# Turns of the modulation vectors: two of 128 rows, or four of 64 in pairs, each half into its own bank

## The chip, the cores and the metric

The program runs on one core of a Trainium2 chip. The metric is the device time of one execution in microseconds (us). The kernel before took 2588.03 us, the median of three runs (2587.11 to 2589.22).

## What is computed

Two stacks of two transformer layers run one after the other on 512 tokens of width 1024, in float32. The first stack has two kinds of attention and a squared-ReLU MLP in each layer. The second stack's layers are modulated by vectors that depend only on a condition `c`:

```python
def second_block(x, c, ada_w, ada_b, ...):
    cond = jax.nn.silu(c)
    for i in range(DEPTH):                      # DEPTH = 2
        mod = cond @ ada_w[i] + ada_b[i]        # [1024] @ [1024, 6144]
        sh1, sc1, g1, sh2, sc2, g2 = jnp.split(mod, N_MOD, axis=-1)
        h = modulate(rmsnorm(x, norm1_g[i]), sh1, sc1)
        ...
```

The change touches the product `cond @ ada_w[i]` alone. It has 2 x 6144 results, each a sum over 1024 inputs.

## The kernel before

The instruction streams of the five engines are written out by hand, each in a function of its own, with semaphores between them; every engine works through its stream in order.

**Large matmuls.** The weights of all products are cut into units of 1024 rows and 256 columns. SyncE loads a unit, ScalarE rounds it into `whi`, GpSimd computes the rest `wlo` (L1891), and TensorE makes two tiles of 128 outputs by 512 tokens from it. A tile is 24 matmuls with 512 columns: for each of 8 chunks of the inner dimension L528 (high times high), L529 (weights high, input low) and L530 (weights low, input high). A tile goes into one of the banks 0 to 3 and is read out by ScalarE or VectorE while the next ones run. All these matmuls use all 128 rows of the array. L622 to L624 are the same in products that are laid out by token.

**An MLP** has eight stages of eight tiles each (`MLP_ORDER`): up, up, down, up, down, up, down, down. In an up stage ScalarE takes ReLU and square of a tile (L1135, L1139), VectorE squares it again in float32 (L1598) and computes the low part (L1601). In a down stage VectorE adds a tile to the residual (L1395, L1397).

**The modulation vectors** need nothing of the tokens, so the product with `ada_w` is worked off beside the first stack's two MLPs, in 48 blocks of 256 outputs, 24 blocks in each MLP, one block for every two tiles:

- SyncE loads the block's 1024 x 256 weights into `ada[k % 2]` (one DMA).
- VectorE (`ada_block(k)`, L1560 and L1563) multiplies eight chunks of 128 rows by the entries of the condition, which stand one to a partition, and adds them up in `acc[k % 2]` (128 partitions, 256 columns). Every step waits for the one before.
- The sum over the 128 partitions is still to be made. TensorE (`ada_sums(k)`, L800 to L807) turns each 128 columns of `acc` with a transpose against the identity: two turns of 128x128, side by side into one bank, 7 or 6 in alternation. `after` calls it behind every even tile from tile 4 to tile 50, so between the last matmul of one tile and the first of the next. TensorE waits there until VectorE's eight steps are done, and until the bank has been read.
- VectorE (`ada_out(k)`, L1565 to L1570) reduces the turned columns, 128 elements per result, adds the bias and writes two columns of `MOD`.

On VectorE the order is `ada_block(k)`, then `ada_out(k - 1)`, then the two tiles' own work. `dve_until` and `pe_until` wait for a semaphore only if a value that high hasn't been waited for before.

**Other short instructions of TensorE.** The attention turns its probabilities in pairs at L691: rows 0 to 63 into bank 4 and rows 64 to 127 into bank 5, each turn 64 rows by 128 columns against a 64x64 identity, and multiplies them by the values at L708. L663 and L671 are its scores, matmuls of 64 rows, also in pairs; while the queries of the second attention are being computed, its first steps stand between large tiles. L918 is one transpose of 48 rows between large tiles, L830 are four of 16 rows, all on the same rows of the array.

Of the kernel before, what the change touches and what calls it, by code (L numbers as in the profile page):

```python
# [7 lines left out]
ALU = mybir.AluOpType  # L8
# [4 lines left out]
P = 128  # L13
# [4 lines left out]
UC = 256  # L18
# [115 lines left out]
def body(nc, ctx, t, consts, out):  # L134
    def sem(name):
        return ctx.enter_context(nc.semaphore(name))

    def sb(name, shape, dt=F32, stack=ctx):
        return stack.enter_context(nc.sbuf_tensor(name, shape, dt))

    bank = [ctx.enter_context(nc.psum_tensor(f"bank{i}", [P, 512], F32)) for i in range(8)]
# [6 lines left out]
    ident, ones = sb("ident", [P, P]), sb("ones", [P, P])  # L148
    head_mean, V2 = sb("head_mean", [P, P]), sb("V2", [P, 96])
# [14 lines left out]
    cond, ada_col = sb("cond", [P, 3, KC]), sb("ada_col", [P, 2, 2])  # L164
    MOD = [sb(f"MOD{i}", [P, 48]) for i in range(2)]
    GM = sb("GM", [P, 4, KC])
    acc = [sb(f"acc{i}", [P, UC]) for i in range(2)]
# [75 lines left out]
    with ExitStack() as region:  # L243
# [11 lines left out]
    hi_done, lo_done, ada_step, ada_sum, ada_red, mod_set, gain_set = (  # L255
        sem(n) for n in ("hi_done", "lo_done", "ada_step", "ada_sum", "ada_red", "mod_set", "gain_set"))
# [164 lines left out]
    def tensor_program(pe):  # L421
# [11 lines left out]
        def wait_chunk(f, c):  # L433
            wait_part(f, KC + c if f in HALVED else c)
# [364 lines left out]
        def mlp(m):  # L799
            def ada_sums(k):  # L800

                pe_until.wait_ge(ada_step, 8 * (k + 1))
                if k >= 2:
                    pe_until.wait_ge(mod_set, k - 1)
                for j in range(2):
                    mm = pe.transpose(bank[7 - k % 2][:, j * P:(j + 1) * P], acc[k % 2][:, j * P:(j + 1) * P], ident[:])
                mm.then_inc(ada_sum, 1)  # L807

            def after(stage, o):
                tile = 8 * stage + o  # L810
                if m < 2 and tile >= 4 and tile % 2 == 0 and tile // 2 - 2 < 24:
                    ada_sums(24 * m + tile // 2 - 2)
            for stage, (f, g) in enumerate(MLP_ORDER):
                name, done = f"m{m}{f}{g}", lambda o, stage=stage: after(stage, o)
                if f == "u":
                    fm(name, X, lambda c: wait_chunk(f"m{m}", c), done, halved=f"m{m}" if g == 0 else None)
                else:
                    fm(name, (Hhi[g % 2], Hlo[g % 2]), lambda c, g=g: pe_until.wait_ge(h_lo, 32 * m + 8 * g + c + 1), done,
                       last=f"m{m}" if g == 3 and m < 3 else None)
# [534 lines left out]
    def vector_program(dve):  # L1354
        dve_until = Until(dve)
# [196 lines left out]
        def ada_block(k):  # L1552

            src, a, cd = ada[k % 2], acc[k % 2], cond[:, 2, :]
            dve_until.wait_ge(ada_in[k % 2], 16 * (k // 2 + 1))
            if k == 0:
                dve_until.wait_ge(silu_step, 3)
            if k >= 2:
                dve_until.wait_ge(ada_sum, k - 1)
            dve.tensor_scalar(a[:], src[:, 0, :], cd[:, 0:1], None, ALU.mult).then_inc(ada_step, 1)  # L1560
            for c in range(1, KC):
                dve_until.wait_ge(ada_step, 8 * k + c)
                dve.scalar_tensor_tensor(a[:], src[:, c, :], cd[:, c:c + 1], a[:], ALU.mult, ALU.add).then_inc(ada_step, 1)  # L1563

        def ada_out(k):  # L1565
            layer, col = k // 24, 2 * (k % 24)
            dve_until.wait_ge(ada_sum, k + 1)
            dve.tensor_reduce(ada_col[:, k % 2, :], bank[7 - k % 2][:, 0:UC].rearrange("p (j k) -> p j k", j=2), mybir.AxisListType.X, ALU.add).then_inc(ada_red, 1)
            dve_until.wait_ge(ada_red, k + 1)
            dve.tensor_tensor(MOD[layer][:, col:col + 2], ada_col[:, k % 2, :], V2[:, 48 * layer + col:48 * layer + col + 2], ALU.add).then_inc(mod_set, 1)  # L1570

        def mod_gains():
            dve_until.wait_ge(mod_set, 48)
# [7 lines left out]
        def mlp(m, gate=None):  # L1581
            for stage, (f, g) in enumerate(MLP_ORDER):
                gm = GEMM[f"m{m}{f}{g}"]
                if m == 1 and stage == 7:
                    mod_gains()
                for o in range(KC - 2 * (m < 3 and stage == 7)):
                    tile = 8 * stage + o
                    if m < 2 and o % 2 == 0 and 2 <= tile < 50:
                        ada_block(24 * m + tile // 2 - 1)
                    if m < 2 and o % 2 == 0 and 4 <= tile < 52:  # L1590
                        ada_out(24 * m + tile // 2 - 2)
                    if f == "u":
                        v = 32 * m + 8 * g + o
                        r = tmp[2 + v % 2]
                        dve_until.wait_ge(up_q, v + 1)
                        if v >= 2:
                            dve_until.wait_ge(h_lo, v - 1)
                        dve.scalar_tensor_tensor(r[:], tmp[v % 2][:], 1.0, tmp[v % 2][:], ALU.mult, ALU.mult).then_inc(up_r, 1)  # L1598
                        dve_until.wait_ge(h_hi, v + 1)
                        dve_until.wait_ge(up_r, v + 1)  # L1600
                        dve.scalar_tensor_tensor(Hlo[g % 2][:, o, :], r[:], 1.0, Hhi[g % 2][:, o, :].bitcast(F32), ALU.mult, ALU.subtract).then_inc(h_lo, 1)  # L1601
                    else:
                        add_to_h(gm.tile + o, o, gate)
                        if g == 3 and m < 3:
                            add_square(f"m{m}", o, 2 if m == 1 else 1)
# [200 lines left out]
        for o in range(GEMM["gv"].tiles):  # L1806
            i, at, g = o % 4, S * (o // 4), GEMM["gv"].tile + o
            if o in (6, 10, 14, 18):
                k = (o - 6) // 4
# [51 lines left out]
        for g in range(3):  # L1861
            for o in range(KC):
                j = 8 * g + o
# [267 lines left out]
```

## Time and profile before

| | |
|---|---|
| median of the runs | 2588.03 us (2587.11 to 2589.22) |
| the profiled execution | 2586.45 us |
| its span in the profile | 2585.1 us |
| TensorE busy | 2539.5 us, 13922 matmuls |
| VectorE busy | 1330.0 us |
| ScalarE busy | 988.4 us |
| GpSimd busy | 1237.2 us |
| DMA | 277.12 MB, mean 107 GB/s |
| L806, turns of the modulation sums | x96, 0.27 us each |
| L1563, VectorE's sums of products | x336, 272.5 us |

The profile is of one execution. PE is TensorE's matmul queue, PEld its weight loads, DVE is VectorE, ACT ScalarE, POOL GpSimd, SP SyncE; L806 is line 806 of the kernel. A matmul's duration reaches from its start until its results are in the bank, and matmuls overlap, so the rate has to be read from the distance between starts. A shape like 64*128 64x64 says that 64 rows and 128 columns of the array are used and that 64 columns of data stream through.

### The profile page before, as it was taken

The numbers are of one execution on the slowest core, as the hardware profiler recorded it, in microseconds if no ns is written. First come the engines' busy times: TensorE is split into PE (matmuls) and PEld (weight loads), VectorE is DVE, ScalarE is ACT, GpSimd is POOL, SyncE is SP. The second block draws the span as 40 slices with busy tenths as digits, with TensorE's granted clock in tenths as the row PEclk, the third lists the DMA queues.
The fourth block names the chain that finished last, engine by engine and source line by source line (L and its number), as shares of the span: only waits on it lengthen the run. The fifth ranks groups of instructions, "written<-read, shape, count | busy, mean of one in ns | idle before, by whom it ended". The sixth has DMA issues, their size and how long they took to land.

```text
span 2585.1 us, 34367 instructions
## 1 busy us (share of the span) xinstructions
PE 2539.5 (98%) x13922; PEld 2083.2 (81%) x13922; DVE 1330.0 (51%) x2303; ACT 988.4 (38%) x1685; POOL 1237.2 (48%) x609
## 2 busy tenths in 40 slices
PE   8989999999999999999999999999999999999999
PEld 5667888888776888888877888888888888888887
DVE  4873999843036599992786532123335223532121
ACT  4474423224347432232577432233324223432231
POOL 4865444443457354444587444444443444444442
PEclk9999999999999999999999999999999999999999
DMA  4111655532320455542310333323322222332321
GB/s 145 53 33 50 202 190 178 188 114 83 98 82 2 129 187 190 195 163 97 116 49 18 98 98 98 98 98 122 115 92 73 97 98 82 97 97 94 99 96 73
DMA packets 260897, 277.12 MB, mean 107 GB/s; under 512 B 7172, under 2 KB 249476, under 8 KB 260484
## 3 DMA queue, kind: packets, MB, share of 16 engines
q1 hardware_dynamic: 259140, 272.31, 32.5%
q8 instruction: 110, 1.80, 0.3%
q10 hardware_dynamic: 1600, 2.62, 0.3%
q14 instruction: 47, 0.39, 0.0%
HBM read 270.19 MB, written 2.10 MB: 105 GB/s over the span
## 4 chain that ended last, share of the span: by engine, by line
PE 87%; DVE 8%; ACT 2%; issue 2%; POOL 1%; DMA 0%; SPq 0%; ACTq 0%; DVEq 0%
PE bank L528 22%; PE bank L529 21%; PE bank L530 21%; DVE acc L1563 2%; PE bank L622 2%; PE bank L623 2%; PE bank L624 2%; PE bank L663 2%; PE bank L708 2%; DVE tmp L1598 2%; PE bank L691 1%; DVE Hlo L1601 1%; PE bank L547 1%; PE bank L487 1%; PE bank L936 1%
## 5 line engine op out<-in xcount | busy, mean ns | idle before, releaser
L1891 POOL TENSOR_TENSOR wlo<-raw,whi 128x1024 fp32r<-128x1024 f32 (+1 forms) x408 | 990.5, 2448 | 1220.3 <-ACT whi L992 1127.4
L992 ACT ACTIVATE whi<-raw 128x1024 fp32r<-128x1024 f32 (+1 forms) x408 | 405.6, 1041 | 575.8 <-PE bank L530 495.9
L528 PE MATMUL bank<-Xhi,whi 128*128 128x512 f32 (+1 forms) x1568 | 620.5, 396 | 1.4 <-POOL wlo L1891 1.4
L529 PE MATMUL bank<-Xlo,whi 128*128 128x512 f32 (+1 forms) x1568 | 611.4, 390 | 0.0
L530 PE MATMUL bank<-Xhi,wlo 128*128 128x512 f32 (+1 forms) x1568 | 610.5, 389 | 0.0
L528 PE MATMUL bank<-Hhi,whi 128*128 128x512 f32 x976 | 381.9, 391 | 0.0
L529 PE MATMUL bank<-Hlo,whi 128*128 128x512 f32 x976 | 380.3, 390 | 0.0
L530 PE MATMUL bank<-Hhi,wlo 128*128 128x512 f32 x976 | 379.7, 389 | 0.0
L528 PEld LDWEIGHTS bank<-Xhi,whi 128*128 128x128 f32 (+1 forms) x1568 | 293.3, 187 | 70.1 <-issue 6.6
L530 PEld LDWEIGHTS bank<-Xhi,wlo 128*128 128x128 f32 (+1 forms) x1568 | 293.4, 187 | 63.7
L529 PEld LDWEIGHTS bank<-Xlo,whi 128*128 128x128 f32 (+1 forms) x1568 | 293.5, 187 | 61.3 <-issue 1.7
L1563 DVE SCALAR_TENSOR_TENSOR acc<-ada,cond,acc 128x256 f32<-128x256 f32 x336 | 272.5, 811 | 12.0
L1397 DVE SCALAR_TENSOR_TENSOR HT<-bank,MOD,HT 128x512 f32<-128x512 f32 x90 | 67.3, 750 | 385.3 <-PE bank L530 365.9
L1598 DVE SCALAR_TENSOR_TENSOR tmp<-tmp 128x512 f32<-128x512 f32 x128 | 136.5, 1066 | 222.5 <-ACT tmp L1135 222.5
L1135 ACT ACTIVATE tmp<-bank 128x512 f32<-128x512 f32 x128 | 76.5, 598 | 411.0 <-PE bank L530 400.1
L530 PEld LDWEIGHTS bank<-Hhi,wlo 128*128 128x128 f32 x976 | 183.3, 188 | 38.5
L528 PEld LDWEIGHTS bank<-Hhi,whi 128*128 128x128 f32 x976 | 183.2, 188 | 37.8
L529 PEld LDWEIGHTS bank<-Hlo,whi 128*128 128x128 f32 x976 | 183.3, 188 | 37.3
L1601 DVE SCALAR_TENSOR_TENSOR Hlo<-tmp,Hhi 128x512 fp32r<-128x512 f32 x128 | 121.1, 946 | 13.6
L1395 DVE TENSOR_TENSOR HT<-bank,HT 128x512 f32<-128x512 f32 x72 | 48.9, 689 | 142.9 <-PE bank L530 142.9
L622 PE MATMUL bank<-whi,Xhi 128*128 128x512 f32 x240 | 94.6, 394 | 0.0
L624 PE MATMUL bank<-whi,Xlo 128*128 128x512 f32 x240 | 93.5, 390 | 0.0
(302 smaller groups left out, 3393.6 us busy)
## 6 DMA issues: line engine op xcount, KB each, us to landing
ada<-in_ada_w SPq DMA_DIRECT2D x48, 1024.0 KB, 5.1
raw<-in_w_up SPq DMA_DIRECT2D x32, 1024.0 KB, 5.4
raw<-in_w_down SPq DMA_DIRECT2D x32, 1024.0 KB, 5.0
raw<-in_mlp_w_in SPq DMA_DIRECT2D x32, 1024.0 KB, 5.3
raw<-in_mlp_w_out SPq DMA_DIRECT2D x32, 1024.0 KB, 5.0
raw<-in_gmlp_w_in SPq DMA_DIRECT2D x24, 1024.0 KB, 5.0
raw<-in_gmlp_w_out SPq DMA_DIRECT2D x12, 1024.0 KB, 5.2
raw<-in_w_in_a SPq DMA_DIRECT2D x8, 1024.0 KB, 5.1
```

The costliest lines, as they stand in the source:

```text
L528: pe.matmul(b[0:rows, :], whi[s][:, c, j:j + rows], hi[:, c, :], start=(c == 0), stop=False)
L529: pe.matmul(b[0:rows, :], whi[s][:, c, j:j + rows], lo[:, c, :], start=False, stop=False)
L530: m = pe.matmul(b[0:rows, :], wlo[s][:, c, j:j + rows], hi[:, c, :], start=False, stop=(c == KC - 1))
L622: pe.matmul(b[:], Xhi[:, c, q * P:(q + 1) * P], hi[:, k, :], start=(c == 0), stop=False)
L624: m = pe.matmul(b[:], Xlo[:, c, q * P:(q + 1) * P], hi[:, k, :], start=False, stop=(c == KC - 1))
L992: act.activation(whi[u % 2][:, c0:c1, 0:k], src[:, c0:c1, 0:k], ACT_F.Copy).then_inc(hi_done, 1)
L1135: act.activation(tmp[v % 2][:], bank[(gm.tile + o) % 4][:], ACT_F.Relu).then_inc(up_q, 1)
L1397: d = dve.scalar_tensor_tensor(HT[:, o, :], b[:], gate[:, o:o + 1], HT[:, o, :], ALU.mult, ALU.add)
L1563: dve.scalar_tensor_tensor(a[:], src[:, c, :], cd[:, c:c + 1], a[:], ALU.mult, ALU.add).then_inc(ada_step, 1)
L1598: dve.scalar_tensor_tensor(r[:], tmp[v % 2][:], 1.0, tmp[v % 2][:], ALU.mult, ALU.mult).then_inc(up_r, 1)
L1601: dve.scalar_tensor_tensor(Hlo[g % 2][:, o, :], r[:], 1.0, Hhi[g % 2][:, o, :].bitcast(F32), ALU.mult, ALU.subtract).then_inc(h_lo, 1)
L1891: pool.tensor_tensor(wlo[u % 2][:, c0:c1, 0:k], src[:, c0:c1, 0:k], whi[u % 2][:, c0:c1, 0:k].bitcast(F32), ALU.subtract).then_inc(lo_done, 1)
```

## The change

The two turns of a block become four. For each 128 columns of `acc` (index `j`) the rows 0 to 63 and the rows 64 to 127 (index `h`) are turned by instructions of their own, each against its 64x64 part of the identity. The two halves go to different banks: bank 4 or 6 for the first, 5 or 7 for the second, by the block's parity. A bank now holds 64 elements per result instead of 128. Both last turns raise `ada_sum`, so its values double. VectorE reduces each bank by itself into its own half of `ada_col`, adds the two halves and then adds the bias. As both halves of `ada_col` are used by every block, it first waits until the block before has been written to `MOD`.

```diff
                 for j in range(2):
-                    mm = pe.transpose(bank[7 - k % 2][:, j * P:(j + 1) * P], acc[k % 2][:, j * P:(j + 1) * P], ident[:])
-                mm.then_inc(ada_sum, 1)
+                    for h in range(2):
+                        r = slice(64 * h, 64 * h + 64)
+                        mm = pe.transpose(bank[4 + 2 * (k % 2) + h][:, 64 * j:64 * j + 64], acc[k % 2][r, j * P:(j + 1) * P], ident[r, r])
+                        if j:
+                            mm.then_inc(ada_sum, 1)
...
             if k >= 2:
-                dve_until.wait_ge(ada_sum, k - 1)
+                dve_until.wait_ge(ada_sum, 2 * k - 2)
...
         def ada_out(k):
             layer, col = k // 24, 2 * (k % 24)
-            dve_until.wait_ge(ada_sum, k + 1)
-            dve.tensor_reduce(ada_col[:, k % 2, :], bank[7 - k % 2][:, 0:UC].rearrange("p (j k) -> p j k", j=2), mybir.AxisListType.X, ALU.add).then_inc(ada_red, 1)
-            dve_until.wait_ge(ada_red, k + 1)
-            dve.tensor_tensor(MOD[layer][:, col:col + 2], ada_col[:, k % 2, :], V2[:, 48 * layer + col:48 * layer + col + 2], ALU.add).then_inc(mod_set, 1)
+            dve_until.wait_ge(ada_sum, 2 * k + 2)
+            if k:
+                dve_until.wait_ge(mod_set, k)
+            for h in range(2):
+                dve.tensor_reduce(ada_col[:, h, :], bank[4 + 2 * (k % 2) + h][:, 0:P].rearrange("p (j k) -> p j k", j=2), mybir.AxisListType.X, ALU.add).then_inc(ada_red, 1)
+            dve_until.wait_ge(ada_red, 3 * k + 2)
+            dve.tensor_tensor(ada_col[:, 0, :], ada_col[:, 0, :], ada_col[:, 1, :], ALU.add).then_inc(ada_red, 1)
+            dve_until.wait_ge(ada_red, 3 * k + 3)
+            dve.tensor_tensor(MOD[layer][:, col:col + 2], ada_col[:, 0, :], V2[:, 48 * layer + col:48 * layer + col + 2], ALU.add).then_inc(mod_set, 1)
```

## Rows read from the trace of the kernel before

**Rows 1.** The page: busy time of each engine; the chain that ended last, by engine.
```profile
PE 2539.5 (98%) x13922; PEld 2083.2 (81%) x13922; DVE 1330.0 (51%) x2303; ACT 988.4 (38%) x1685; POOL 1237.2 (48%) x609
...
PE 87%; DVE 8%; ACT 2%; issue 2%; POOL 1%; DMA 0%; SPq 0%; ACTq 0%; DVEq 0%
```

**Rows 2.** Line L806: duration min/median/max in ns; what TensorE waited for.
```profile
L806 PE MATMUL bank<-ident,acc x96: 270/271/327, 289.9 to 1166.6; 128*128 128x128 f32 x96
...
  DVE acc L1563: 5.1, 4
```

**Rows 3.** TensorE's timeline at two blocks (start us, duration us, line, shape).
```profile
289.62 0.39 PE L530 MATMUL bank<-Xhi,wlo 128*128 128x512 f32 x1
289.85 0.38 PE L806 MATMUL bank<-ident,acc 128*128 128x128 f32 x2
...
290.31 0.40 PE L529 MATMUL bank<-Xlo,whi 128*128 128x512 f32 x1
...
300.79 0.39 PE L530 MATMUL bank<-Xhi,wlo 128*128 128x512 f32 x1
```

**Rows 4.** The same in a later MLP without blocks, 48 matmuls apart.
```profile
1515.31 0.39 PE L530 MATMUL bank<-Xhi,wlo 128*128 128x512 f32 x1
...
1526.19 0.39 PE L530 MATMUL bank<-Xhi,wlo 128*128 128x512 f32 x1
```

**Rows 5.** TensorE's timeline at L918, one turn of 48 rows.
```profile
1911.59 0.39 PE L624 MATMUL bank<-whi,Xlo 128*128 128x512 f32 x1
1911.91 0.26 PE L918 MATMUL bank<-ident,tmp 48*128 48x48 f32 x1
...
1912.43 0.39 PE L623 MATMUL bank<-wlo,Xhi 128*128 128x512 f32 x1
```

**Rows 6.** TensorE's timeline at L830, four turns of 16 rows.
```profile
684.01 0.39 PE L624 MATMUL bank<-whi,Xlo 128*128 128x512 f32 x1
684.33 0.42 PE L830 MATMUL bank<-ident,FT 16*128 16x16 f32 x4
...
685.02 0.40 PE L623 MATMUL bank<-wlo,Xhi 128*128 128x512 f32 x1
```

**Rows 7.** TensorE's timeline where score matmuls of 64 rows stand between tiles.
```profile
747.71 0.39 PE L530 MATMUL bank<-Xhi,wlo 128*128 128x512 f32 x1
748.02 0.49 PE L663 MATMUL bank<-KB,QB 64*128 64x128 f32 x4
...
748.85 0.39 PE L529 MATMUL bank<-Xlo,whi 128*128 128x512 f32 x1
...
753.83 0.39 PE L530 MATMUL bank<-Xhi,wlo 128*128 128x512 f32 x1
```

**Rows 8.** TensorE's timeline in the attention: groups of paired 64-row turns.
```profile
780.88 0.53 PE L691 MATMUL bank<-ident,PBB 64*128 64x64 f32 x12
781.34 0.44 PE L708 MATMUL bank<-TB,VB 128*64 128x128 f32 x4
...
782.90 0.65 PE L691 MATMUL bank<-ident,PBB 64*128 64x64 f32 x16
783.49 0.66 PE L708 MATMUL bank<-TB,VB 128*64 128x128 f32 x8
```

**Rows 9.** Busy us (instructions) of PE, PEld, DVE, ACT, POOL; clock, DMA share, GB/s.
```profile
277.00:369.00 92.00, 91.17 (x408) 74.74 (x406) 88.29 (x105) 33.42 (x45) 48.27 (x18) 1.00 0.61 197
```

**Rows 10.** VectorE's timeline in an up stage.
```profile
353.45 0.42 DVE L1568 TENSOR_REDUCE ada_col<-bank 128x2 f32<-128x256 f32 x1
353.90 0.16 DVE L1570 TENSOR_TENSOR MOD<-ada_col,V 128x2 f32<-128x2 f32 x1
353.99 2.89 DVE L1598 SCALAR_TENSOR_TENSOR tmp<-tmp 128x512 f32<-128x512 f32 x1
...
359.61 0.68 DVE L1598 SCALAR_TENSOR_TENSOR tmp<-tmp 128x512 f32<-128x512 f32 x1
```

**Rows 11.** TensorE's timeline at block 7, with its wait.
```profile
369.23 0.44 PE L806 MATMUL bank<-ident,acc 128*128 128x128 f32 x2 [1.06 <-DVE acc L1563]
```

## The prediction

> **What bounds the kernel now.** I read the page first, its busy times and its chain. TensorE is busy for 98% of the span of 2585.1 us and holds 87% of the chain that ended last, VectorE only 8% [rows 1]. So an edit is worth what it does to the time between TensorE's instructions, and work on another engine counts only where TensorE waits for it. Next I read the line that is edited. The 48 blocks of modulation vectors make 96 turns of 128x128 at L806; TensorE waited for VectorE's sums in front of them 5.1 us, its load and matmul queues added, 4 times in all [rows 2]: two blocks of the 48, then. Then the timeline around one block, because durations mislead here: a turn is shown with 0.27 us, yet two of them, one behind the other, push the next large matmul back by less than that. What counts is the distance between starts.
>
> **What a block costs today.** My measure is the "seam": from the start of the last matmul of one tile to the start of the second matmul of the next. With nothing between them it is two steps. One step is (1526.19 - 1515.31) / 48 = 0.2267 us [rows 4], two are 0.45. With today's two turns the seam runs from 289.62 to 290.31, or 0.69 [rows 3]: the turns cost 0.24. A full period of two tiles and one block, 289.62 to 300.79, is 11.17 [rows 3], against 48 x 0.2267 = 10.88 without a block [rows 4]: 0.29 in all, so 0.05 more is lost in steps that run slightly late behind the seam. The 48 blocks cost about 48 x 0.29 = 13.9 us together, which is the most that any edit of them could win.
>
> **What the change removes and adds on TensorE.** Two turns that use all 128 rows of the array become four that use 64: per column half one on rows 0 to 63 and one on rows 64 to 127. The attention's turns (L691) have just this form, so their pace is in the trace. A group of 12 takes 0.46 us up to the next instruction, a group of 16 takes 0.59 [rows 8]: four more cost 0.13, a pair 0.065. The two pairs would be 0.13 where the two turns are now 0.24. If that were all, a block would win 0.11.
>
> It is not all, since in attention the instructions in front of the turns use 64 rows too. Here the turns stand between matmuls that use 128 rows, and the trace shows what happens where instructions of fewer rows are put there. Ahead of the one 48-row turn of L918 the last matmul starts at 1911.59 and the turn at 1911.91, 0.32 later instead of 0.23, and the seam is 1912.43 - 1911.59 = 0.84 [rows 5]. Ahead of four turns of 16 rows (L830) the gap is again 0.32 and the seam is 685.02 - 684.01 = 1.01 [rows 6]. Ahead of the 64-row score matmuls it is 748.02 - 747.71 = 0.31, and the seam is 748.85 - 747.71 = 1.14, with six wider instructions in it [rows 7]. A single small turn thus costs 0.84 - 0.45 = 0.39, more than two big ones side by side with the stream (0.24). The gap is the same before three different lines with different waits, so I read it as a price of going from the whole array to part of it, with a second price on the way back. The present turns never leave the whole array and pay neither.
>
> What the Trainium skill (TensorEngine Tiling (Array Packing), Key Properties) says of this is "Changing tiling mode (not just tile) drains the TensorE"; it gives no time for it, and the 0.32 us gaps agree. Its section Theoretical Speedup promises "up to 2x" for sides of 64 or less, which the pace inside the attention's groups bears out and the seams do not.
>
> The new seam is not in the trace, so I bound it. It can't be below 0.84, since it holds more turns than the one of L918. It is hardly above 1.01: four 16-row turns of L830 all share the same rows of the array, so they can't run side by side. I build the value from the nearest row, L918: 0.84, plus one more pair 0.065 [rows 5, 8], plus 0.02, my estimate for a first turn of 64 rows and columns instead of 48 (0.065 grown in the ratio 64 to 48 is 0.022 more). That is 0.925, or 0.235 more than today's 0.69; the bounds are 0.15 and 0.32 more.
>
> The late steps behind the seam cost 0.05 now (from 290.31 to 300.79 there are 46 steps in 10.48 us, against 10.43). Behind the 64-row group none is lost: 748.85 to 753.83 is 22 steps in 4.98, against 4.99 [rows 7]. They may stay or vanish; I take half, -0.02, with ends of -0.05 and 0.
>
> Sum on TensorE: 48 x (0.235 - 0.02) = +10.3 us. Low end 48 x (0.15 - 0.05) = +4.8, high end 48 x 0.32 = +15.4.
>
> **What the change adds on VectorE.** One reduction of 256 columns (0.42 us) becomes two of 128 and a sum of two columns; the addition to MOD (0.16 us) stays [rows 10]. A half reduction isn't in the trace; it costs between 0.16 (the smallest instruction there) and 0.42. I take 0.28, midway, and as they don't depend on each other the second starts before the first is done, as L1598 starts 0.09 behind the 0.16 us of L1570 [rows 10]. Together: 0.28 + 0.21 + 0.16 + 0.03 of semaphore, where 0.42 + 0.03 stood: about +0.25 us a block, ends -0.1 and +0.6. In most blocks VectorE's idle time hides it. The new wait on mod_set (block k's reductions wait for block k-1's last addition, as both halves share ada_col now) is met a whole period earlier and costs nothing; queued behind it would be the additions and the squares of the tile. The MLP's up stages are the exception: from 277 to 369 us VectorE is busy 88.29 of 92 us [rows 9], and at the end of that stretch TensorE waits 1.06 us for the last sum of block 7 [rows 11]. The second of the two blocks that wait is the one at the same place of the other MLP [rows 2]. The granted clock is 1.00 there, 2.4 GHz [rows 9], and I expect no change of it. Up to that sum VectorE has done six read-outs, +1.5 us; TensorE itself arrives there 7 x 0.215 = 1.5 us later. They cancel, and I leave both waits as they are: 0. Ends: both waits vanish (-2.1), or each grows by about 2.
>
> **Banks.** The turns move from banks 6 and 7 to 4 to 7. No other work uses banks 4 and 5 while blocks run (their next use is the last unit of the MLP, after the last block), so nothing waits for that: 0.
>
> **Sum.** The profiled execution took 2586.45 us, 1.35 over its span. 2586.45 + 10.3 = 2596.75. The three runs' median, 2588.03, stands 1.58 above the profiled one; on its scale the forecast is 2598.3 us.
>
> **Rivals.**
> - *The switch is free here (the other side).* The weights of the 64-row turns might be loaded while the last 128-row matmul still streams, as the whole-array turns' are now. Then only the pace counts: 0.13 for 0.24, 48 x -0.11 = -5.3, 2582.7 us, faster by 0.2%. It decides at whether the first 64-row load waits for the matmul ahead. For it: those three lines each have a semaphore wait in front, which could be what held them. Against: the same 0.31 to 0.32 at all of them, while L806 waits for a semaphore too and starts 0.23 behind the matmul [rows 3, 5 to 7]. The Trainium skill (TensorE: Matmul & The Clock Gate, The mechanism) states the rule for this case: a weight load is pulled ahead of running matmuls when its rows don't conflict or when it goes to the background buffer. The groups' rows here do not show it across a change of height. Chance 0.08.
> - *VectorE takes over in the up stages.* The same square (L1598) that takes 0.68 us at 359.61 took 2.89 at 353.99, when GpSimd worked too [rows 10], so one that slips into GpSimd's time costs 2.2 more. If that happens once in either MLP, the two waits of 1.06 grow to about 3.2 and the total is 2598.3 + 4.3 = 2602.6. For it: VectorE has no slack there. Against: GpSimd starts on TensorE's tiles, and shifts along with them. Chance 0.10.
> - *The halves don't run side by side.* Then each of four turns costs 0.065 by itself, and a block 0.13 more: 2598.3 + 6.2 = 2604.5. Against: in attention they do, into two banks as here. Chance 0.05.
>
> **How the numbers follow.** Forecast 0.77. About 5.2 us (0.2%) is what a measurement of this kernel can tell from no change. Of the forecast's share 0.04 lies below +5.2, since its low end is +4.8 and the waits could go as well. Of the free switch half lies beyond -5.2. That gives faster 0.04, same 0.08, slower 0.88. The range: from the low end (+4.8, less most of 2.1) to the high end (+15.4, with a part of the waits), 2591 to 2605.5 us; it leaves out the free switch and the corners.
>
> **What would show it.** Between the last 512-column matmul and the first turn 0.32 instead of 0.23 us; a seam of about 0.92 instead of 0.69; a period of 11.38 instead of 11.17 in both MLPs with blocks; the same step of 0.2267 and the same times everywhere else. On VectorE about 0.8 us a read-out instead of 0.54. The wait ahead of block 7 at about 1 us. A first turn 0.23 behind the matmul would prove the forecast wrong and the free switch right; a seam of 0.92 with an unchanged total would mean that TensorE had slack that I don't see.

## The result and the profile after

The changed kernel took 2598.68 us, the median of five runs (2597.13 to 2599.18), against 2588.03 for the kernel before (2587.11 to 2589.38). The ratio is 1.0039, with a 95% interval from 1.0028 to 1.0050: slower by 7.2 to 12.9 us. The forecast was 2598.3 us.

The page after, its span, busy times and chain, answers to [rows 1]:

```profile
span 2597.2 us, 34702 instructions
...
PE 2555.2 (98%) x14018; PEld 2084.4 (80%) x14018; DVE 1337.8 (52%) x2399; ACT 988.5 (38%) x1685; POOL 1238.7 (48%) x609
...
PE 94%; ACT 2%; DVE 2%; issue 1%; POOL 1%; DMA 0%; SPq 0%; ACTq 0%; DVEq 0%
```

TensorE now holds 94% of the chain where it held 87%, VectorE 2% instead of 8%. That by itself does not say that TensorE is slower; it says that where VectorE's up stages and TensorE's matmuls ran level, VectorE is no longer the last. TensorE's timeline at the first two blocks answers to [rows 3]:

```profile
291.41 0.39 PE L530 MATMUL bank<-Xhi,wlo 128*128 128x512 f32 x1
291.73 0.34 PE L808 MATMUL bank<-ident,acc 64*128 64x64 f32 x4
292.00 0.50 PE L528 MATMUL bank<-Xhi,whi 128*128 128x512 f32 x1
292.34 0.40 PE L529 MATMUL bank<-Xlo,whi 128*128 128x512 f32 x1
...
302.83 0.39 PE L530 MATMUL bank<-Xhi,wlo 128*128 128x512 f32 x1
```

The same place in the kernel before has this row for the large matmul behind the turns:

```profile
289.99 0.48 PE L528 MATMUL bank<-Xhi,whi 128*128 128x512 f32 x1
```

The first turn starts 0.32 us behind the last matmul, not 0.23. The four turns take 0.27 up to the next matmul, where the two took 289.99 - 289.85 = 0.14, and that matmul holds its place for 0.34, where it held it for 0.32. The seam is 292.34 - 291.41 = 0.93 where it was 0.69, and the period is 11.42 where it was 11.17. It is so at all 48 blocks.

The weight loads (PEld) show where the 0.32 begins. The turns' loads before:

```profile
289.62 0.37 PEld L806 LDWEIGHTS bank<-ident,acc 128*128 128x128 f32 x2
```

And after:

```profile
291.73 0.20 PEld L808 LDWEIGHTS bank<-ident,acc 64*128 64x128 f32 x4 [0.35 <-issue]
```

Before, the first load starts together with the last large matmul (289.62), 0.23 us ahead of its own turn. After, it starts only with its own turn, 0.32 behind the last large matmul, and the load queue is idle for 0.35 us ahead of it. This too is the same at all 48 blocks, apart from blocks 7 and 31 of the kernel before, where TensorE waited.

The wait for block 7 is gone. At this place [rows 11] had 1.06 us:

```profile
371.31 0.39 PE L530 MATMUL bank<-Hhi,wlo 128*128 128x512 f32 x1
371.63 0.34 PE L808 MATMUL bank<-ident,acc 64*128 64x64 f32 x4
```

VectorE's timeline ahead of it answers to [rows 10]:

```profile
344.80 0.48 DVE L1574 TENSOR_REDUCE ada_col<-bank 128x2 f32<-128x128 f32 x2
...
345.50 0.16 DVE L1578 TENSOR_TENSOR MOD<-ada_col,V 128x2 f32<-128x2 f32 x1
345.59 0.69 DVE L1606 SCALAR_TENSOR_TENSOR tmp<-tmp 128x512 f32<-128x512 f32 x1
...
364.68 5.63 DVE L1566 SCALAR_TENSOR_TENSOR acc<-ada,cond,acc 128x256 f32<-128x256 f32 x7
```

This read-out takes 345.59 - 344.80 = 0.79 us, where one took 353.99 - 353.45 = 0.54. (The next one, from 356.52 to 359.51, takes 2.99: its last addition runs beside GpSimd and has 2.36 instead of 0.16.) The seven additions of block 7 are done at 370.31, a microsecond before TensorE asks for them at 371.31.

**Where the time went.** With the periods of the two profiles: 48 x (11.413 - 11.167) = +11.8 us, and the two long waits gone, -2.5 us (a period with one lasted 12.43 before). Sum +9.3, inside the measured interval. The two profiled spans differ by 12.1. The other 2.8 lie outside the blocks, in parts of the program that the change does not touch: 1.8 before the first block and 1.1 behind the last. The first 30 us of the execution after ran in part at a lower granted clock, as this view of it shows (stretch, its length, busy us and instructions of PE, PEld, DVE, ACT, POOL, then the granted clock as a share of 2.4 GHz, DMA share and GB/s):

```profile
0.00:30.00 30.00, 19.33 (x75) 15.55 (x76) 11.99 (x26) 17.32 (x27) 10.27 (x11) 0.94 0.54 178
```

The same 30 us of the execution before have 1.00. That is a difference of two executions, and I put none of it to the change.

### The profile page after: what moved, and what is told of

Same layout as the page of the kernel before. It is cut to its first block, busy times and chain, and to the rows that moved or that the text cites. A ratio compares the mean times of both kernels' runs of the same rounds, so it can differ in the third digit from the quotient of the medians.

```text
span 2597.2 us, 34702 instructions
## 1 busy us (share of the span) xinstructions
PE 2555.2 (98%) x14018; PEld 2084.4 (80%) x14018; DVE 1337.8 (52%) x2399; ACT 988.5 (38%) x1685; POOL 1238.7 (48%) x609
## 4 chain that ended last, share of the span: by engine, by line
PE 94%; ACT 2%; DVE 2%; issue 1%; POOL 1%; DMA 0%; SPq 0%; ACTq 0%; DVEq 0%
PE bank L528 24%; PE bank L529 23%; PE bank L530 23%; PE bank L708 2%; PE bank L663 2%; PE bank L622 2%; PE bank L624 2%; PE bank L623 2%; PE bank L691 1%; PE bank L547 1%; PE bank L487 1%; PE bank L939 1%; PE bank L548 1%; PE bank L549 1%; PE bank L478 1%
```

## Experiments

Theory S: the array's switch from 128 rows to 64 and back has a price of its own at every seam, larger than what the pairs win. The rivals differ from run to run. All ratios are to the kernel before, measured beside each group of runs.

**e1_vector_part.** The kernel before with VectorE's part of the change alone.

```diff
+            if k:
+                dve_until.wait_ge(mod_set, k)
+            for h in range(2):
+                dve.tensor_reduce(ada_col[:, h, :], bank[7 - k % 2][:, 0:UC].rearrange("p (j k) -> p j k", j=2)[:, :, 64 * h:64 * h + 64], ...)
...
+            dve.tensor_tensor(ada_col[:, 0, :], ada_col[:, 0, :], ada_col[:, 1, :], ALU.add)
```

> TensorE as before (two turns of 128 rows into one bank), VectorE as after (two reductions of 64 elements per result, the addition of the halves, the wait on mod_set). Theory S (the time goes into switching the array between 128 and 64 rows): seams stay at 0.69 us, the period at 11.17, and only the two waits at blocks 7 and 31 (1.06 us each) can move, to between 0 and 2.6 each: 2586 to 2591 us. Rival V (VectorE's longer read-out is what costs): most of the +10.7 us appears here, about 2598 us, with TensorE waiting for VectorE at many blocks.

Measured: 2588.89 us, ratio 1.0002 (0.9993 to 1.0012). The seams stay at 0.69. The waits at blocks 7 and 31 grew; this is the one at block 7:

```profile
366.30 0.39 PE L530 MATMUL bank<-Hhi,wlo 128*128 128x512 f32 x1
368.39 0.44 PE L806 MATMUL bank<-ident,acc 128*128 128x128 f32 x2 [1.70 <-DVE acc L1563]
```

Rival V falls. VectorE's longer read-out costs two waits of 1.70 us instead of 1.06 while TensorE keeps its old pace; in the changed kernel, where TensorE is slower, there is no wait.

**e3_no_turns.** The kernel before with the wait at each seam but without a turn.

```diff
-                for j in range(2):
-                    mm = pe.transpose(bank[7 - k % 2][:, j * P:(j + 1) * P], acc[k % 2][:, j * P:(j + 1) * P], ident[:])
-                mm.then_inc(ada_sum, 1)
...
-            dve.tensor_reduce(ada_col[:, k % 2, :], ...)
+            dve.tensor_tensor(MOD[layer][:, col:col + 2], acc[k % 2][:, 0:2], V2[...], ALU.add)
```

> The kernel before without any turn and without the reduction (MOD gets the bias plus two columns of the unsummed products, so the sums over partitions are left out); TensorE still waits for each block's sums at the same place. It measures what 48 blocks cost TensorE in all. Theory S's base: seam 0.45, period 10.88 if the late steps behind a seam come with the turns, 10.93 if they come with the wait; 48 x 0.29 = 13.9 us less than before, and the two waits gone or nearly: 2572 to 2575 us.

Measured: 2573.55 us, ratio 0.9942 (0.9925 to 0.9958). The period is 10.88, as in an MLP without blocks:

```profile
400.42 0.39 PE L530 MATMUL bank<-Xhi,wlo 128*128 128x512 f32 x1
...
411.30 0.39 PE L530 MATMUL bank<-Xhi,wlo 128*128 128x512 f32 x1
```

So a semaphore that is met costs nothing at a seam, and the late steps behind it come with the turns.

**e2_one_pair.** The changed kernel with one pair of turns a block instead of two.

```diff
-                for j in range(2):
-                    for h in range(2):
-                        ...
+                for h in range(2):
+                    r = slice(64 * h, 64 * h + 64)
+                    pe.transpose(bank[4 + 2 * (k % 2) + h][:, 0:64], acc[k % 2][r, 0:P], ident[r, r]).then_inc(ada_sum, 1)
```

> The changed kernel with only the first 128 of a block's 256 columns turned: one pair of 64-row turns instead of two, each bank reduced twice over the same columns (the other columns' vectors are left out, so half of MOD is wrong). Theory S: the two switches stay, only a pair's 0.062 goes: seam 0.865 instead of 0.927, period 11.35, about -3 us from the changed kernel, 2595.7 us. Rival N (the price goes with the number of turns): half the turns, half the 0.47 us, seam 0.69, -11 us, about 2587 us.

Measured: 2594.24 us, ratio 1.0025 (1.0014 to 1.0036).

```profile
291.56 0.39 PE L530 MATMUL bank<-Xhi,wlo 128*128 128x512 f32 x1
291.88 0.28 PE L807 MATMUL bank<-ident,acc 64*128 64x64 f32 x2
...
292.43 0.40 PE L529 MATMUL bank<-Xlo,whi 128*128 128x512 f32 x1
```

The seam is 0.87 by these rows (0.86 in the median of all), the gap 0.32. Half of the turns gone takes 0.06 to 0.07 off the 0.93, not 0.24: rival N falls. The waits at blocks 7 and 31 stand again here, with 1.1 us each, and are part of the total. This kernel turns half of what the kernel before turns and is still slower than it.

**e5_same_rows.** The changed kernel with all four turns on rows 0 to 63.

```diff
-                        r = slice(64 * h, 64 * h + 64)
+                r = slice(0, 64)
```

> The changed kernel with all four turns on rows 0 to 63 (rows 64 to 127 of the sums are left out, the first half is counted twice). Theory S: the two switches stay and the pairs can no longer run side by side; from the four 16-row turns of the trace (seam 1.01 against 0.84 for one) each further turn costs 0.057: seam 0.865 + 2 to 3 x 0.057 = 0.98 to 1.04, +3 to +5 us on the changed kernel, 2601 to 2604 us. Rival: the pairs never ran side by side here, then seam and time stay at 0.927 and 2598.7 us.

Measured: 2602.0 us, ratio 1.0056 (1.0041 to 1.0071). The seam is 301.97 - 300.92 = 1.05, 0.12 more than with the pairs on both halves:

```profile
300.92 0.39 PE L530 MATMUL bank<-Xhi,wlo 128*128 128x512 f32 x1
301.24 0.46 PE L808 MATMUL bank<-ident,acc 64*128 64x64 f32 x4
...
301.97 0.40 PE L529 MATMUL bank<-Xlo,whi 128*128 128x512 f32 x1
```

So the pairs of the changed kernel do run side by side, and that wins 0.06 us a pair. What they win is real and is less than the switch.

**e6_full_twice.** The kernel before with its two turns made twice.

```diff
+                for h in range(2):
-                for j in range(2):
+                    for j in range(2):
-                    mm = pe.transpose(bank[7 - k % 2][...], acc[k % 2][...], ident[:])
+                        mm = pe.transpose(bank[7 - k % 2 - 2 * h][...], acc[k % 2][...], ident[:])
```

> The kernel before with its two 128-row turns made twice, the second time into another bank that nobody reads: four turns as after, but the whole array throughout. Theory S: the first turn stays 0.23 behind the large matmul, each turn costs 0.11: seam 0.69 + 0.22 = 0.91, about +10.5 us on before, 2598.5 us. Rival I (four instructions, their loads or the second bank make the gap): the first turn starts 0.32 behind the large matmul, as after.

Measured: 2594.98 us, ratio 1.0027 (1.0016 to 1.0038), where 2598.5 was expected.

```profile
289.94 0.39 PE L530 MATMUL bank<-Xhi,wlo 128*128 128x512 f32 x1
290.17 0.60 PE L807 MATMUL bank<-ident,acc 128*128 128x128 f32 x4
...
290.84 0.40 PE L529 MATMUL bank<-Xlo,whi 128*128 128x512 f32 x1
```

Rival I falls: four instructions and a second bank leave the gap at 0.23. The seam is 0.90, as expected. What my total left out is that TensorE, 0.2 us later at each block, no longer meets the two waits of block 7 and block 31; with them the sum is 48 x 0.205 - 2.5 = +7.3. So twice the work of the kernel before, on 128 rows, has a shorter seam (0.90) than that work done once on 64 rows (0.93). The totals, +7.0 and +10.65, point the same way, but their intervals overlap.

**e4_ones.** The kernel before with each 128 columns of `acc` as the weights of a float32 matmul against one column of ones.

```diff
-                    mm = pe.transpose(bank[7 - k % 2][:, j * P:(j + 1) * P], acc[k % 2][:, j * P:(j + 1) * P], ident[:])
+                    mm = pe.matmul(bank[7 - k % 2][:, j:j + 1], acc[k % 2][:, j * P:(j + 1) * P], ones[:, 0:1], start=True, stop=True)
...
-            dve.tensor_reduce(ada_col[:, k % 2, :], bank[7 - k % 2][:, 0:UC]..., ALU.add).then_inc(ada_red, 1)
```

> The kernel before, with the sum over the 128 partitions made on TensorE: each 128 columns of the products are the weights of a float32 matmul against one column of ones, so that no turn, no reduction and no ada_col are left; VectorE adds the bias straight from the bank. All of it on 128 rows, so no switch. Theory S: no gap, first short matmul 0.23 us behind the large one, two at the 0.09 us of the row sums of squares (L448, four in 0.37): seam 0.63 to 0.65 instead of 0.69, 2 to 3 us less; VectorE is 0.45 us a block shorter, so the waits at blocks 7 and 31 go: -2.1. Together 2583 to 2584 us. Rival: a float32 matmul of one column costs as much as a turn of 128 (0.11), then only the waits go: 2586 us.

Measured: 2596.28 us, ratio 1.0033 (1.0020 to 1.0045): 12 us worse than expected, and outside both guesses.

```profile
300.70 0.40 PE L530 MATMUL bank<-Xhi,wlo 128*128 128x512 f32 x1
300.94 0.50 PE L806 MATMUL bank<-ones,acc 128*128 128x1 f32 x4
...
301.62 0.39 PE L529 MATMUL bank<-Xlo,whi 128*128 128x512 f32 x1
```

The code makes two matmuls a block and the trace shows four, with four weight loads: each float32 matmul is two instructions, while a turn is one. I had read L448's "four in 0.37" as four matmuls of the code; they were two. The seam of 0.92 is that of four full turns, though only one column streams through, so the number of streamed columns does not set their price. That the four weight loads do is my reading; no run tests it alone.

**e7_one_switch_for_two.** The changed kernel with the turns of two blocks (0+1, 2+3, ...) behind every second slot.

```diff
+                if k % 2 == 0:
+                    return
...
+                for n in (k - 1, k):
                     for j in range(2):
                         for h in range(2):
+                            r, at = slice(64 * h, 64 * h + 64), 128 * (n % 2) + 64 * j
+                            mm = pe.transpose(bank[4 + 2 * (k // 2 % 2) + h][:, at:at + 64], acc[n % 4][r, j * P:(j + 1) * P], ident[r, r])
```

> The changed kernel with the turns of two blocks made together behind every second slot (eight 64-row turns in four pairs), so that the array is switched 24 times instead of 48; same results. Theory S: one seam of 0.45 and one of 0.927 + 2 x 0.062 = 1.05 for every two blocks instead of two of 0.927: 0.35 less, and half of the late steps (0.05) with it: 24 x 0.35 to 0.40 = 8.4 to 9.6 us less than the changed kernel, 2589 to 2590.5 us. Rival N (the price goes with the number of turns): no difference from the changed kernel, 2598.7 us.

Measured: 2599.62 us, ratio 1.0042 (1.0028 to 1.0056). The total supports rival N, the seams support theory S:

```profile
300.68 0.39 PE L530 MATMUL bank<-Xhi,wlo 128*128 128x512 f32 x1
301.00 0.46 PE L811 MATMUL bank<-ident,acc 64*128 64x64 f32 x8
...
301.74 0.40 PE L529 MATMUL bank<-Xlo,whi 128*128 128x512 f32 x1
```

Eight turns in a seam of 1.06, and a period of 22.42 for two blocks against 22.83 in the changed kernel: 9.8 us saved over 24 seams. It is given back at blocks 7 and 31, here at block 7:

```profile
367.92 0.39 PE L530 MATMUL bank<-Hhi,wlo 128*128 128x512 f32 x1
371.15 0.69 PE L811 MATMUL bank<-ident,held 64*128 64x64 f32 x8 [2.84 <-DVE held L1569]
...
372.36 0.63 PE L529 MATMUL bank<-Hlo,whi 128*128 128x512 f32 x1
372.79 0.63 PE L530 MATMUL bank<-Hhi,wlo 128*128 128x512 f32 x1
```

TensorE waits 2.84 us for VectorE, and behind the wait its steps are 0.43 instead of 0.23. The periods that hold these waits last 28.22 and 27.97 us, 5.8 and 5.6 more than the others: 11.4 us for the two.

**e8_pairs_off_block7.** The same with the pairs 1+2, 3+4, ..., so that block 7 is turned one slot later, with block 8.

```diff
+    def ada_group(k):
+        n = k % 24
+        if n == 0 or n == 23:
+            return (k,)
+        return (k - 1, k) if n % 2 == 0 else ()
```

> Again 64-row turns of two blocks behind one seam, but the pairs are blocks 1+2, 3+4, ... of each MLP (0 and 23 alone), so that no seam needs the sum of block 7 or 31 on time, where the version with pairs 0+1, 2+3, ... waited 2.9 us twice and then ran at half the granted clock. Same results. Theory S (the switches are the price, and the last version only lost its gain to those waits): 22 seams of 1.05 and 4 of 0.93, together 15.0 us over bare seams plus about 1.2 of late steps, against 25.6 in the changed kernel: -9.4 us, 2589.3 us, about the kernel before. Rival G (what a longer seam saves is lost again behind it, wherever it stands): no gain, 2596 to 2600 us.

Measured: 2590.78 us, ratio 1.0011 (1.0002 to 1.0020). That is 7.9 us under the changed kernel (8.7, each against the kernel before as measured beside it) with the same turns and the same results: rival G falls. It is still slower than the kernel before, by 0.5 to 5.2 us. The seams of two blocks are 335.73 - 334.68 = 1.05:

```profile
334.68 0.39 PE L542 MATMUL bank<-Xhi,wlo 128*128 128x512 f32 x1
335.00 0.34 PE L824 MATMUL bank<-ident,held 64*128 64x64 f32 x4
335.18 0.29 PE L824 MATMUL bank<-ident,acc 64*128 64x64 f32 x4
...
335.73 0.40 PE L541 MATMUL bank<-Xlo,whi 128*128 128x512 f32 x1
...
979.72 0.34 PE L824 MATMUL bank<-ident,acc 64*128 64x64 f32 x4 [2.63 <-DVE held L1582]
```

My claim that no wait would be left was wrong: one of 1.16 us stands at block 8 and one of 2.63 in the second MLP, at the seam of blocks 29 and 30 (last row), so the late ones moved and did not vanish.

**e9_full_pairs.** The same grouping with the 128-row turns of the kernel before.

```diff
+                for n in ada_group(k):
+                    g, i = ada_place(n)
+                    for j in range(2):
+                        at = 256 * i + 128 * j
+                        mm = pe.transpose(bank[7 - g % 2][:, at:at + 128], acc[n % 4][:, j * P:(j + 1) * P], ident[:])
```

> The same grouping with the 128-row turns of the kernel before: four turns behind one seam, into one bank. Same results. Theory S: without a switch there is little to save by grouping: 22 x 0.45 + 4 x 0.23 + 1.2 = 12.0 us against 13.7 before, and the two waits (2.5) go since blocks 7 and 31 are not needed so early: -4.2 us, 2583.8 us, faster than both kernels. If grouping saved a fixed price per seam here too, as with 64 rows, it would be -4.2 - 22 x 0.3 = about 2577 us.

Measured: 2582.53 us, ratio 0.9976 (0.9966 to 0.9986): faster than both kernels, with the same results.

```profile
309.84 0.39 PE L542 MATMUL bank<-Xhi,wlo 128*128 128x512 f32 x1
310.07 0.38 PE L823 MATMUL bank<-ident,acc 128*128 128x128 f32 x2
...
310.74 0.40 PE L541 MATMUL bank<-Xlo,whi 128*128 128x512 f32 x1
```

The seam of two blocks holds four turns and is 0.90, twice 0.22 over a bare one: on 128 rows there is no fixed price that grouping could save. The period of two blocks is 22.25 against 22.33, 1.8 us over 22 of them. TensorE never waits for the sums, another 2.5. Together 4.3, inside the measured gain of 3.6 to 8.8 us; where the rest of its middle, 6.3, comes from I did not test.

**e10_quarters.** The changed kernel with turns of 32 rows, four to each 128 columns.

```diff
-                    for h in range(2):
-                        r = slice(64 * h, 64 * h + 64)
+                    for h in range(4):
+                        r = slice(32 * h, 32 * h + 32)
```

> The changed kernel with four turns of 32 rows for each 128 columns instead of two of 64, each quarter into its own bank, VectorE reducing four banks. Same results. Theory S (a fixed price for leaving the whole array and coming back, not one for the height): gap 0.32 again and a seam of 0.93 to 0.95, if four run side by side; 1.05 if only two do. VectorE has about 0.45 us more to do in each block, so the waits at blocks 7 and 31 come back, 0 to 3 us each: 2599 to 2606 us. Rival H (the price grows as the pieces get smaller): gap over 0.32 or seam over 1.1.

Measured: 2610.49 us, ratio 1.0087 (1.0071 to 1.0102).

```profile
290.41 0.39 PE L530 MATMUL bank<-Xhi,wlo 128*128 128x512 f32 x1
290.73 0.32 PE L808 MATMUL bank<-ident,acc 32*128 32x32 f32 x8
...
291.31 0.40 PE L529 MATMUL bank<-Xlo,whi 128*128 128x512 f32 x1
```

The gap is 0.32 again and the seam 0.90, slightly less than with 64 rows: rival H falls, the price is one for leaving the whole array. The total is above my range (2599 to 2606) for other reasons. The first I had built in: with four banks to a block there is no second set, and TensorE waits for VectorE to have read the block before. Its waits say so (engine, line, waited for: us in total, times, longest):

```profile
PE bank L808 <- DVE MOD L1580: 11.0, 8, 2.0
```

The second I had not foreseen: behind the longest of these waits, one in each MLP, the granted clock fell. The periods that hold them last 14.99 and 14.92 us instead of 11.35, 1.6 more than the wait itself (last section).

**The seams together.** All are distances from the last matmul of a tile to the second of the next, medians over the seams of a run; the rows above can differ from them by 0.01, by rounding.

| between the tiles | first gap | seam |
|---|---|---|
| nothing | 0.23 | 0.45 |
| 2 turns, 128 rows | 0.23 | 0.69 |
| 4 turns, 128 rows (e6, e9) | 0.23 | 0.90 |
| 2 turns, 64 rows, one pair (e2) | 0.32 | 0.86 |
| 4 turns, 64 rows, two pairs (after) | 0.32 | 0.93 |
| 8 turns, 64 rows, four pairs (e7, e8) | 0.32 | 1.05 |
| 4 turns, 64 rows, all on the same rows (e5) | 0.32 | 1.05 |
| 8 turns, 32 rows, two fours (e10) | 0.32 | 0.90 |

With 64 rows these seams fit 0.80 + 0.063 for each pair, with 128 rows 0.45 + 0.11 for each turn. One pair does the work of one turn, so it wins 0.05 and the switch costs 0.35. By these two lines the pairs would pay from about seven full turns behind one another. That is an estimate beyond what was measured: the longest islands here are four pairs (1.05) and four turns (0.90). A block has two turns.

## Why the prediction was right, point by point

- **The switch.** The gap of 0.32 and the seam of 0.925, built from L918 and the attention's pace, were measured as 0.32 and 0.93. The bounds 0.84 and 1.01 held. e2, e6, e7, e8 and e10 show that the price is paid for each change to part of the array, whatever the number of turns behind it.
- **The rule and the rows.** "Changing tiling mode (not just tile) drains the TensorE" (the Trainium skill, TensorEngine Tiling (Array Packing), Key Properties) agrees with every gap of the table. The runs do not show what the array does in that time; they show its length, 0.09 us more before the first turn and the rest of the 0.35 behind it. The free switch of my first rival fell at all 48 seams: the load of the first 64-row turn starts 0.32 behind the last large matmul, that of the first 128-row turn together with it. The rule of the Trainium skill (TensorE: Matmul & The Clock Gate, The mechanism), by which a weight load is pulled ahead when its rows don't conflict or it goes to the background buffer, agrees with the 128-row turns of this trace and does not hold across this change of height.
- **Side by side.** The third rival fell with e5: on the same rows the seam grows by 0.12.
- **The late steps** (0.05 in all) were to lose half. They did not: 11.413 - 10.88 = 0.53, less 0.47 for the seam, leaves 0.06, where 0.03 was forecast. The period grew by 0.246 instead of 0.215, 1.5 us in all, of which 1.2 are the late steps and 0.3 the seam. e3 shows that they come with the turns, not with the wait; what makes them I don't know.
- **VectorE.** The read-out at 0.79 us instead of 0.54 is what I worked out (+0.25). The waits at blocks 7 and 31 I left at 1.06 each; they went, -2.5 us, at the end of my range for them and a bit beyond. The step that failed is "they cancel". Counted from the last large matmul before the first turns (289.62 and 291.41), block 7's seven additions start 1.5 us later than before (73.27 against 71.77) and TensorE arrives 1.7 later, much as in the sum. But the additions themselves got shorter. These are the additions and GpSimd's work beside them before, and then GpSimd's work after:

```profile
361.39 7.79 DVE L1563 SCALAR_TENSOR_TENSOR acc<-ada,cond,acc 128x256 f32<-128x256 f32 x7
363.97 4.92 POOL L1891 TENSOR_TENSOR wlo<-raw,whi 128x1024 fp32r<-128x1024 f32 x2 [4.83 <-ACT whi L992]
```

```profile
367.49 5.07 POOL L1899 TENSOR_TENSOR wlo<-raw,whi 128x1024 fp32r<-128x1024 f32 x2 [5.06 <-ACT whi L995]
```

  Seven additions take 3.61 us where GpSimd is idle (from 353.00 in the execution after, for instance), and one that runs beside it takes about 2.1 more. Before, GpSimd started 2.58 us behind the first of the seven, and two of them met it: 7.79. After, it started 367.49 - 364.68 = 2.81 behind, and one did: 5.63. So VectorE was done 0.7 us earlier instead of 1.5 later, and a shift of 0.23 us against GpSimd decided it, by these rows of one execution each. e1 shows the other half of the pair: with VectorE later and TensorE not, the wait is 1.70. The second rival, that VectorE takes over, did not come true in the changed kernel; waits near its size stand in e7 (2.84) and, at one seam, in e8 (2.63).
- **The sum.** +10.3 was forecast; the profile's periods and waits give +9.3, the runs' medians +10.65. The errors of the two terms, +1.5 and -2.5, went against each other, and the remaining 1.35 between +9.3 and +10.65 is not in the blocks, so the closeness of the total is in part luck; that of the seam is not.

## What to carry to other kernels

Before splitting small TensorE work into row groups, look at what runs before and behind it: if that uses all 128 rows, each island of smaller height costs a fixed time, here 0.35 us, and by the estimate above it must hold about seven full turns of work to win it back. Grouping islands saves that price; grouping work that never leaves the whole array saves next to nothing by itself (here 0.08 us for two blocks), but can move a wait away from a place where another engine is late. And price an insertion by the distance between the starts of its neighbours, from a place in the trace where the heights change in the same way.

## What the runs showed of the hardware that I had not expected

- Behind the wait of 2.84 us in e7 TensorE's granted clock went to the lower level, 1.2 GHz, for part of the next stretches. TensorE had been busy without a break before the wait. The stretches, columns as above:

```profile
366.00:370.00 4.00, 2.31 (x11) 1.57 (x9) 3.93 (x3) 0.00 (x0) 3.25 (x2) 1.00 0.00 0
370.00:374.00 4.00, 2.85 (x13) 2.32 (x14) 3.82 (x9) 0.00 (x0) 0.00 (x0) 0.59 0.40 126
374.00:378.00 4.00, 4.00 (x12) 3.07 (x11) 3.68 (x14) 0.00 (x0) 0.00 (x0) 0.56 1.08 379
```

  So a wait of 2.84 us made its period 5.8 us longer. A shorter wait can do it too: in e10 one of 1.96 us ended at 362.70, and the steps from 364.29 on were 0.43 instead of 0.23:

```profile
364.00:368.00 4.00, 4.00 (x12) 3.18 (x11) 3.72 (x8) 0.00 (x0) 0.00 (x0) 0.57 0.69 242
```

  But in e8 a wait of 2.63 us at 977 was followed by a clock of 1.00, and so was one of 1.8 us at 324 in e10. The length of the wait alone does not decide it; what does I can't say from these runs.
- A float32 matmul of the code is two instructions with two weight loads on TensorE, a float32 turn is one. With one column streaming, four such instructions cost the seam as much as four turns of 128 columns (0.92 and 0.90).
